# The halves of keys and queries exchanged by DMA instead of by a product with a rotation matrix

## The reference, cut to what matters

```python
def _apply_rope(x, cos, sin):
    half = ATTN_HEAD_DIM // 2
    rot = jnp.concatenate([-xf[..., half:], xf[..., :half]], axis=-1)
    return xf * cos + rot * sin

def _hybrid_layer(...):
    pl = _project(hl, w_in)                          # latent tokens
    a_l = _conv_branch(pl, ...)                      # 31 taps, normalised, SiLU
    q_l = _apply_rope(_heads(pl['b_q'], 8), cos, sin)
    k_l = _apply_rope(_heads(pl['b_k'], 2), cos, sin)
    b_l = _windowed_attention(q_l, k_l, v_l, k_cx, v_cx, attn_sink) * silu(pl['b_gate'])
    c_l = gated linear attention
    xl = xl + gate * (concat(a_l, b_l, c_l) @ w_out)
```

## Time and profile before

| | |
|---|---|
| median of 3 runs | 3666.86 us (3666.4 to 3673.7) |
| profiled execution | 3664.23 us |
| its span | 3662.4 us |
| TensorE matmul / weight load busy | 3491.9 (95%) / 2795.2 us (76%) |
| VectorE / ScalarE / GpSimd busy | 1863.2 (51%) / 931.6 (25%) / 1815.1 us (50%) |
| mean granted TensorE clock | 0.985 of full speed |

### The profile page before, as it was taken

The page is one execution under the profiler, slowest core; times in us unless marked ns, Lnnn a source line. Parts: engine busy times, 40 slices in busy tenths (PEclk is TensorE's granted clock), DMA queues, the critical chain, the costliest instruction groups (busy, mean ns, idle before and its releaser), DMA issues.

```text
span 3662.4 us, 49453 instructions
## 1 busy us (share of the span) xinstructions
PE 3491.9 (95%) x19612; PEld 2795.2 (76%) x19612; DVE 1863.2 (51%) x2551; ACT 931.6 (25%) x1503; POOL 1815.1 (50%) x1826
## 2 busy tenths in 40 slices
PE   5998997999899799999999999999999999999998
PEld 3786786778678677777788888876777778888886
DVE  5684825559481556335543444355434553443346
ACT  4113534321363433133211011113223221111111
POOL 3342014567302477547744445457745864444445
PEclk9999998999999899999999999999999999999999
DMA  5510010331001143213211111114322311111113
GB/s 211 213 52 12 2 37 25 107 124 58 18 2 43 39 153 127 65 51 118 89 48 43 55 52 38 58 44 138 99 57 74 122 55 55 48 39 58 48 37 100
DMA packets 87607, 257.57 MB, mean 70 GB/s; under 512 B 9808, under 2 KB 12880, under 8 KB 86608
## 3 DMA queue, kind: packets, MB, share of 16 engines
q1 hardware_dynamic: 70896, 216.65, 18.4%
q10 hardware_dynamic: 16480, 37.76, 3.5%
HBM read 229.20 MB, written 16.78 MB: 67 GB/s over the span
## 4 chain that ended last, share of the span: by engine, by line
PE 79%; DVE 11%; POOL 5%; ACT 2%; issue 1%; DMA 1%; SPq 0%; DVEq 0%; POOLq 0%; ACTq 0%
PE banks L683 22%; PE banks L685 21%; PE banks L684 21%; POOL w_lo L2428 4%; DVE wk L1920 3%; PE banks L799 2%; PE banks L813 2%; PE banks L832 2%; DVE nt L1825 1%; POOL w_hi L2425 1%; DVE wk L2076 1%; DVE h_lo L1838 1%; DMA gw<-w_mod 1%; PE banks L827 1%; DVE nt L1814 1%
## 5 line engine op out<-in xcount | busy, mean ns | idle before, releaser
L683 PE MATMUL banks<-h_hi,w_hi 128*128 128x512 f32 (+1 forms) x3488 | 1357.0, 389 | 14.4 <-POOLq L2433 13.2
L685 PE MATMUL banks<-h_hi,w_lo 128*128 128x512 f32 (+1 forms) x3488 | 1335.4, 383 | 0.0
L684 PE MATMUL banks<-h_lo,w_hi 128*128 128x512 f32 (+1 forms) x3488 | 1333.0, 382 | 0.0
L2428 POOL TENSOR_TENSOR w_lo<-raw,w_hi 128x256 fp32r<-128x256 f32 x1320 | 1270.0, 990 | 31.2
L2425 POOL CAST w_hi<-raw 128x1024 fp32r<-128x1024 f32 (+2 forms) x390 | 398.1, 1021 | 1641.1 <-PE banks L685 1179.7
L683 PEld LDWEIGHTS banks<-h_hi,w_hi 128*128 128x128 f32 x3488 | 655.4, 188 | 164.7 <-POOLq L2433 26.6
L684 PEld LDWEIGHTS banks<-h_lo,w_hi 128*128 128x128 f32 x3488 | 655.4, 188 | 136.5 <-issue 7.4
L685 PEld LDWEIGHTS banks<-h_hi,w_lo 128*128 128x128 f32 x3488 | 654.9, 188 | 134.3
L2373 DVE TENSOR_SCALAR nt<-wk,v 128x1024 f32<-128x1024 f32 x88 | 90.1, 1024 | 462.0 <-ACTq L1757 435.6
L1536 ACT ACTIVATE wk<-banks 128x512 f32<-128x512 f32 x200 | 118.9, 595 | 706.6 <-PE banks L685 681.5
L683 PE MATMUL banks<-g_hi,w_hi 128*128 128x512 f32 x704 | 280.4, 398 | 11.5 <-DVEq L2362 6.4
(11 more groups left out here) (232 smaller groups left out, 3409.7 us busy)
## 6 DMA issues: line engine op xcount, KB each, us to landing
raw<-w_in SPq DMA_DIRECT2D x118, 512.0 KB, 3.5
raw<-w_ffn SPq DMA_DIRECT2D x96, 512.0 KB, 3.5
raw<-w_out SPq DMA_DIRECT2D x64, 512.0 KB, 3.5
raw<-w_down SPq DMA_DIRECT2D x96, 256.0 KB, 2.6
x<-w_mod SPq DMA_DIRECT2D x16, 1024.0 KB, 7.0
wk<-residual ACTq DMA_DIRECT2D x42, 256.0 KB, 3.1
gw<-w_mod SPq DMA_DIRECT2D x4, 2048.0 KB, 20.5
residual<-x ACTq DMA_DIRECT2D x4, 2048.0 KB, 9.4
```

Of the source, the lines that this page charges most:

```text
L683: mm(o, wh[:, ws], hi[:, at_, t0:t0 + n], start=kt == 0, stop=False)
L684: mm(o, wh[:, ws], lo[:, at_, t0:t0 + n], start=False, stop=False)
L685: last = mm(o, wl[:, ws], hi[:, at_, t0:t0 + n], start=False, stop=kt == nk - 1)
L2428: last = G.tensor_tensor(w_lo[:, piece], raw[:, piece], w_hi[:, piece].bitcast(F32), ALU.subtract)
```

## The change

`rotate` and the matrix `rot` go, and with them `rot_ready`. Behind each raw tile ScalarE now issues four DMAs (`swap_halves`) that copy the halves crosswise into one of two buffers `at_sw` of 128x1024 in `nt`, and `rope` works from that buffer: one product with the sine (its sign is now in the table, as rows of -sin and +sin) and one addition, each over 1024 tokens and with both inputs in SBUF. From m = 2 on `swap_halves` first waits for `rope_ready` of the rope two tiles before. The next writer of a raw buffer waits for the DMAs that read it in place of `rot_ready`. The constants become 128 columns narrower.

```diff
--- before.py
+++ after.py
@@ -125,15 +125,10 @@
 
     s, t = np.arange(P)[:, None], np.arange(P)[None, :]
     same = (s // 64) == (t // 64)
-    rot = np.zeros((P, P))
-    for h in (0, 64):
-        for i in range(32):
-            rot[h + 32 + i, h + i] = -1.0
-            rot[h + i, h + 32 + i] = 1.0
     kj = np.arange(384)[None, :]
     local = np.where(np.abs(P + np.arange(P)[:, None] - kj) <= P, 0.0, -1e30)
     heads = (np.arange(P)[:, None] // GD) == (np.arange(256)[None, :] // 64)
-    parts = [("ident", np.eye(P)), ("rot", rot), ("ones", np.full((P, P), 1.0 / D)),
+    parts = [("ident", np.eye(P)), ("ones", np.full((P, P), 1.0 / D)),
              ("ones256", np.full((P, P), 1.0 / 256)),
              ("ones64", ((s // 64) == (t // 64)) / 64.0),
              ("cumf", (same & (s <= t)) / 16.0), ("cumb", (same & (s >= t)) / 16.0),
@@ -180,7 +175,7 @@
     ang2 = np.concatenate([ang2] * 4, 1).T
     first = np.where(np.arange(P)[:, None] % HD < HD // 2, f32(-1), f32(1))
     return [np.ascontiguousarray(x, dtype=f32) for x in
-            (np.concatenate([np.cos(ang), np.sin(ang)], 1), np.concatenate([np.cos(ang2), first * np.sin(ang2)], 1))]
+            (np.concatenate([np.cos(ang), first * np.sin(ang)], 1), np.concatenate([np.cos(ang2), first * np.sin(ang2)], 1))]
 
 
 CONST_AT, CONSTS = masks()
@@ -298,6 +293,7 @@
     assert a.at <= 3 * T + 2 * (S + C + 4 * PAD)
     a = Area(nt, 0, 3840)
     at_mask = a.take(896)
+    at_sw = [nt[:, a.at + i * S:a.at + (i + 1) * S] for i in range(2)]
     at_p = [a.take(SLOT) for _ in range(2)] + [at_raw_[:, 0:SLOT]]
     at_col = a.take(32)
     at_s, at_p = [[b.rearrange("p (g c) -> p g c", g=2) for b in bufs] for bufs in (at_s, at_p)]
@@ -364,7 +360,7 @@
         act_step dve_step pool_step
         glu_ready u_ready conv_ready mean_ready cent_ready csq_ready var_ready csd_ready cn_ready csilu_ready
         gate_ready mixc_ready 
-        raw_ready rot_ready cosm_ready rope_ready vt_ready vn_ready vz_ready
+        raw_ready swap_in0 swap_in1 cosm_ready rope_ready vt_ready vn_ready vz_ready
         sc_ready nmax_ready exp_ready rec_ready pt_ready pta_copied ptd_copied o_ready mixa_ready
         z_ready zabs_ready sp_ready la_ready turned v_copied kt_copied cum_ready ex_ready dec_ready kd_ready kin_ready
         gu_ready gu_copied gst_ready gsc_ready gmask_ready gam_ready pv_ready go_ready goa_copied god_copied
@@ -438,7 +434,14 @@
     PAIR1 = [len(PAIRS[0]), len(PAIRS[0]) + len(PAIRS[1])]
 
     CONV_BANKS = (3, 4, 7)
-    ROT_BANKS = (5, 6)
+
+    def raw_of(m):
+
+        return at_raw[0 if m == 0 else (m - 1) % 2]
+
+    def swaps(l, m):
+
+        return 64 * ((3 - m % 2) * l + m // 2 + 1)
 
     def keys_of(n):
 
@@ -749,18 +752,6 @@
                     if l == 0:
                         modulate_late(name)
 
-                def rotate(m):
-
-                    n = 5 * l + m
-                    pe.wait_ge(sem["raw_ready"], n + 1)
-                    if n:
-                        pe.wait_ge(sem["rope_ready"], n)
-                    raw = at_raw[0 if m == 0 else (m - 1) % 2]
-                    for ci in range(2):
-                        last = mm(psum[ROT_BANKS[ci]], k("rot"), raw[:, ci * 512:(ci + 1) * 512], start=True, stop=True)
-                    last.then_inc(sem["rot_ready"], 1)
-
-                rotate(0)
                 pe.wait_ge(sem["vt_ready"], l + 1)
                 pe.wait_ge(sem["mod_ready"], 2)
                 for t in range(NTT):
@@ -781,8 +772,6 @@
                 last.then_inc(sem["var_ready"], 1)
                 for j in range(1, 4):
                     project(proj_index(l, f"q{j}"), h_hi, h_lo)
-                    rotate(j)
-                rotate(4)
 
                 pairs = PAIRS[l]
 
@@ -1313,17 +1302,29 @@
                 def mix_gate(j):
                     evacuate(proj_index(l, f"bg{j}"), lambda t0, w: x[:, 2 + j, t0:t0 + w], ACT.Silu)
 
+                def swap_halves(m):
+
+
+                    if m >= 2:
+                        act.wait_ge(sem["rope_ready"], 5 * l + m - 1)
+                    q = HD // 2
+                    for o in range(0, P, HD):
+                        for to, of in ((o, o + q), (o + q, o)):
+                            act.dma_start(at_sw[m % 2][to:to + q, :], raw_of(m)[of:of + q, 0:S]).then_inc(sem[f"swap_in{m % 2}"], 16)
+
                 def raw_query(j):
 
                     if j != 1:
-                        n = 5 * l + max(j - 1, 0)
-                        act.wait_ge(sem["rot_ready"], n + 1)
-                        act.wait_ge(sem["cosm_ready"], n + 1)
+                        m = max(j - 1, 0)
+                        act.wait_ge(sem[f"swap_in{m % 2}"], swaps(l, m))
+                        act.wait_ge(sem["cosm_ready"], 5 * l + m + 1)
                     evacuate(proj_index(l, f"q{j}"), lambda t0, w: at_raw[j % 2][:, t0:t0 + w], ACT.Copy)
                     act.sem_inc(sem["raw_ready"], 1)
+                    swap_halves(j + 1)
 
                 evacuate(proj_index(l, "bk"), lambda t0, w: at_raw[0][:, t0:t0 + w], ACT.Copy)
                 act.sem_inc(sem["raw_ready"], 1)
+                swap_halves(0)
                 copy_late("bk")
                 evacuate(proj_index(l, "bv"), lambda t0, w: at_raw[1][:, t0:t0 + w], ACT.Copy)
                 act.sem_inc(sem["vt_ready"], 1)
@@ -1936,13 +1937,11 @@
 
                 def rope(m, dst):
 
-                    n = 5 * l + m
-                    dve.wait_ge(sem["rot_ready"], n + 1)
-                    dve.wait_ge(sem["cosm_ready"], n + 1)
-                    for ci in range(2):
-                        sl, b = slice(ci * 512, (ci + 1) * 512), psum[ROT_BANKS[ci]]
-                        link(V.tensor_tensor(b, b, at_cs[:, S + ci * 512:S + (ci + 1) * 512], ALU.mult))
-                        link(V.tensor_tensor(dst[:, sl], dst[:, sl], b, ALU.add))
+                    dve.wait_ge(sem["rope_in"], 16 * (l + 1))
+                    dve.wait_ge(sem[f"swap_in{m % 2}"], swaps(l, m))
+                    link(V.tensor_tensor(at_sw[m % 2], at_sw[m % 2], at_cs[:, S:2 * S], ALU.mult))
+                    dve.wait_ge(sem["cosm_ready"], 5 * l + m + 1)
+                    link(V.tensor_tensor(dst[:, 0:S], dst[:, 0:S], at_sw[m % 2], ALU.add))
                     dve.sem_inc(sem["rope_ready"], 1)
 
                 rope(0, at_k)
@@ -2446,7 +2445,7 @@
                 def cosines(m, dst):
 
                     n = 5 * l + m
-                    raw = at_raw[0 if m == 0 else (m - 1) % 2]
+                    raw = raw_of(m)
                     pool.wait_ge(sem["raw_ready"], n + 1)
                     pool.wait_ge(sem["rope_in"], 16 * (l + 1))
                     if m >= 2:
```

## The result

The changed kernel takes 3678.31 us (median of 8 runs, 3675.25 to 3683.51) against 3666.70 us of the kernel before on the same chip (8 runs, 3665.43 to 3673.70): a ratio of 1.0029, 95% interval 1.0018 to 1.0040, so about 11 us slower. The profiled executions took 3677.88 and 3664.23 us, spans 3676.1 and 3662.4; they differ by 13.7 us, 2 more than the medians, so some 2 us of what follows belong to this pair of executions and not to the change. The prediction was 3668.1 with 3675 as its upper end, and "within 0.2%" as the likeliest case. Both missed: the change costs ten times what was forecast.

What follows compares the result with a forecast made beforehand. TensorE was busy 95% of the span, but waits on ScalarE, VectorE and GpSimd were taken to bind around the removed rotations. Layer 0's -2.4 and layer 1's +3.6 gave +1.2 us: 3668.1 against the median, range 3657 to 3675.

Steps and rivals of the forecast that it cites:

- forecast 2.5 + 4.3: Layer 0, behind q1's copy: four DMA issues take 2.5 us, then the table load and SiLUs end 4.3 us later.
- the layer-1 chain +1.0: Layer 1, before q3: issues, SiLUs and a product end 7.7 us after q1's copy, making the chain 1.0 us later.
- forecast 5.0: Layer 1, before L774: TensorE's idle gap grows from 3.28 to 5.0 us.
- The first two rivals: Issuing hardly holds ScalarE, 3657 us, chance 0.10; TensorE is the bound throughout, 3647 us, chance 0.04.
- Bounds 0 and 1.6 ... I take +1.6: Slower clock after TensorE's idle gaps at q3 in both layers and before L774 in layer 1: +1.6 us each.
- +1.1 us: Layer 0, late modulation: the keys' swap issues delay ScalarE's copies, so TensorE goes on 1.1 us later.
- The ends, "-3.6" and "-2.0": From q3's last copy to the first masked scores: 7.4 us, so -3.6 in layer 0 and -2.0 in layer 1.
- The disturbance, "I take 1.4": Before q3, each layer: VectorE's two-input SBUF products slow GpSimd's split of q3's weights by 1.4 us, upper bound 2.5.
- for the one beside the cosine product: Before q3: the 1.4 us of disturbance counts less for the VectorE instruction running beside GpSimd's cosine product.
- Rotation 0 saves nothing: Layer 1: the convolution on VectorE sets when L774 runs, so removing the first rotation gains 0.
- passes to the end: After each stretch comes attention, fed by what ends there, so the sum of +1.2 us reaches the kernel's end.
- The third rival: GpSimd's queue before q3 and rope 4: GpSimd and VectorE exclude each other, issues slower; +7.9 us, 3675, chance 0.09.

Runs made afterwards that it cites:

- changed_again: The changed kernel run once more, nothing altered; 3678.84 us, 1.0028 of the kernel before.
- reorder: The changed kernel, but ScalarE issues the keys' swap behind the late-modulation copies and q1's swap behind the two SiLUs; 3667.38 us, ratio to before 1.0000.
- delay: The changed kernel, but VectorE's third rope (q1's) waits until GpSimd has split q3's weights; 3674.67 us, ratio to before 1.0018.
- order_only: The changed kernel with the edits of reorder and delay together, no unread products; 3664.56 us, ratio to before 0.9989.
- on_sp: The changed kernel with the same 40 transfers issued by SyncE instead of ScalarE; 3667.22 us, ratio to before 0.9998.
- fill: The changed kernel plus 19 unread TensorE products in its waits (late modulation, before L765's second half in layer 1, before q3); 3668.51 us, ratio to before 1.0002.
- dead: The changed kernel plus unread products in four of the rotation's five places per layer; ScalarE's overwriting waits for them; 3675.98 us, ratio to before 1.0016.
- combo: The changed kernel with reorder, delay and unread products before L765's second half and q3 (layer 1) and behind the first scores (both layers); 3653.86 us, 0.9960 of before.
- combo_sp: As combo, but SyncE issues the swaps at their first places (on_sp and delay instead of reorder and delay); 3648.70 us, ratio to before 0.9948.
- before_tail: The kernel before plus unread products, 3 ahead of the last rotation and 4, 2, 2 behind the first three scores per layer; 3663.75 us, ratio 0.9988.
- held: The kernel before, with ScalarE also issuing the swaps of keys, q0, q1 and q2, whose result nobody reads; 3668.45 us, ratio 1.0002.

## Why the prediction was wrong

Right: the chain. Issues at 612 ns (514/612/2126), 2.45 us for four, behind each copy; SiLUs 6.8 us behind q1's copy in layer 0 (forecast 2.5 + 4.3); the layer-1 chain +1.0; gaps before q3 in both layers with GpSimd as releaser; the gap before L765 5.67 (forecast 5.0). The first two rivals needed the opposite of each. The rule of the Trainium skill, "DMA: Bandwidth & Descriptors", section "Issuing engines are not separate DMA queues", that an issue is usually small beside its DMA, was rightly set aside: 2.45 us for four issues beside a landing of 2.3.

Wrong, by the steps of the sum:

1. **"Bounds 0 and 1.6 ... I take +1.6"**, the clock. This term was priced from one row (3.33 less 1.72) as if a drop cost only the four records right behind the gap, and the 1.6 was called an upper bound. It measured 2.0, 2.6 and 2.4 at its three places; and at the late modulation, where "+1.1 us" was taken as a wait alone, another 1.7 behind a gap of 1.14. Together 8.7 where 4.8 stood: +3.9.
2. **The ends, "-3.6" and "-2.0"**: -2.6 and +0.1, so +3.1. VectorE's two products took 3.2 to 3.4 us, not 2.9, and in layer 1 one issue took 2.13 us. The maximum of 1812 ns stood in the earlier trace rows; I weighed against it that "most of the issues are near their median", but the one long issue lay on the path. It is no accident of one execution: in six of the ten traces in which the last swap is issued (changed, changed_again, reorder, delay, order_only, on_sp), one issue of that swap in layer 1 takes 1.4 to 2.1 us. In fill, dead, combo and combo_sp none does; why is open.
3. **The disturbance, "I take 1.4"**: 1.7 and 2.7 against twice 1.4, +1.6. The ratio of the earlier trace rows was right (2.1 lost for 2.91, 0.71; here 1.8 for 2.45); the discount "for the one beside the cosine product" was not, that one cost 0.8. And in layer 1 a third product, rope 3's at 967.58, fell on the split and cost 0.95. By the rule of the Trainium skill, "SBUF — State Buffer", section "Who interferes with whom" (whole instructions exclude each other), it would be 2.5 and 3.7 us: the sign and the place agree, the size, an estimate from that rule, is over a third too large, and the measured one decides.
4. "Rotation 0 saves nothing" in layer 1, convolution unchanged: it ended 0.7 late, its VectorE taps beside the same split.
5. What follows each stretch "passes to the end": +2.7 arose elsewhere, 1.7 of it between the stretches, where two drops at 602 and 797 us are longer (2.7 and 2.9 us lost, before 1.5 and 1.4). These are not the change's own: reorder has 2.7 at 789, before_tail, which keeps the rotations, 2.6 at 792, held 1.5 at 797. The gaps ahead of the later one are nearly the same in both (1.05, 2.10, 1.14 us against 1.06, 2.09, 1.34); where the drop falls among them differs. That this is chance is likely, since the medians differ by only 11.6 us, and not shown.

3.9 + 3.1 + 1.6 + 0.7 + 2.7 = 12.0, and the forecast's +1.2: 13.2 of 13.7; the rest is 0.1 or 0.2 in several places. The third rival, "GpSimd and VectorE shut each other out", had the sign and most of the place at 3675, but gave it 0.09; it left out the clock, which every one of its delays brings along. That was the error of the range: the costs were bounded singly, though a longer wait and a lower clock come together.

In the words of the experiments: the loss goes away with the hold of ScalarE ahead of urgent work (reorder and on_sp, 11 us each), or with the idle clock (fill, 10 us), and in part with the disturbance (delay, about 4). They don't add up to one sum: a shorter wait also spares clock, and a filled one spares clock at the same length. How much of the 11 us is wait and how much clock, these runs don't say.

## What to carry to other kernels

A DMA issue is work of the engine that issues it: put it on a queue with nothing urgent behind it, or behind what is urgent. When work is taken from TensorE in a stretch where it waits for others, price the idle time twice, once as the wait and once as the clock that follows it, at what the rows at the lower level show for everything up to the recovery; and look at whether unread products in the waits give it back. Remove a cover only after seeing what it covered.

## What the runs showed of the hardware

- A gap of 1.14 us in a thin stretch (rows of two columns) was followed by a grant at the lower level for part of 183 to 191 us (0.79), worth 1.7 us (0.62 and 3.4 us in delay); the drop came in the changed kernel, its repetition, dead, delay and held, where the copy waits, and in none of the others, where it is prompt or a product stands in the gap.
- Two-input VectorE products in SBUF: the neighbour on GpSimd loses 0.8 to 1.0 us per product of 1.22 (cosine product 2.4 to 3.2, cast 1.04 to 2.04), while VectorE may lose nothing (1.22 and 1.23) or much (3.32 beside 3.31 in delay; 2.77 at 312.55 us in the changed kernel, beside a cosine product that took its usual 2.37). In the kernel before, VectorE instructions with an operand in PSUM (L1944 and L1945, from 309.79 us) ran beside a cosine product that began at 308.65 and took 2.37 us, undisturbed. The exchange by DMA thus moved VectorE's work from a kind that leaves GpSimd alone to one that doesn't.
- An issue is 0.61 us at the median on ScalarE and 0.59 on SyncE, but on both the longest of 40 was 2.1 us, each time in the last swap of layer 1; in four of ten traces no issue of that swap is long (at most 0.61 us).
